# Projections dealt between the mLSTM heads, and adaLN products with the weights as stationary operand, in a hybrid decoder step

## What is computed

```
mod = silu(c) @ w_mod + b_mod            # 9 sequences, 6*1024 columns: shift, scale, gate, twice
h   = RMSNorm(x) * (1 + scale1) + shift1
z   = h @ w_in                           # conv x_c, B, C | mLSTM q, k, v, o (512 columns each) | gates i, f
y_c = B * dwconv3_causal(C * x_c)        # state: last 2 rows of C*x_c
y_m = o * mLSTM(q, k, v, i, f)           # 4 heads of 128, states C, n, m
x   = x + gate1 * ([GroupRMSNorm(y_c) | HeadRMSNorm(y_m)] @ w_out)
h   = RMSNorm(x) * (1 + scale2) + shift2
x   = x + gate2 * PEER(h)                # 8 heads, 16384 experts; then the final RMSNorm
```

## Time and profile before

| | us |
|---|---|
| median of 3 executions | 1919.88 (1917.03 to 1927.48) |
| the profiled execution | 1925.03 |
| its span in the trace | 1923.3 |
| PE busy, share of the span | 1801.0, 94% |
| DVE / ACT / POOL busy | 1368.4 / 682.4 / 1131.1 |

### The profile page before, as it was taken

The page is one execution under the profiler, slowest core; times in us unless marked ns, Lnnn a source line. Parts: engine busy times, 40 slices in busy tenths (PEclk is TensorE's granted clock), DMA queues, the critical chain, the costliest instruction groups (busy, mean ns, idle before and its releaser), DMA issues.

```text
span 1923.3 us, 27208 instructions
## 1 busy us (share of the span) xinstructions
PE 1801.0 (94%) x10594; PEld 1717.0 (89%) x10594; DVE 1368.4 (71%) x2341; ACT 682.4 (35%) x864; POOL 1131.1 (59%) x617
## 2 busy tenths in 40 slices
PE   8999985887999999999999999998999999999995
PEld 3899973576999999999999998998999999999995
DVE  2436006545789699987777877637989999999965
ACT  2453422133323333335444454433333333333331
POOL 2666622012325788865444444467878888888861
PEclk9999987978999999999999999998999999999998
DMA  8544352131204788866877787689999999999961
GB/s 315 166 147 143 131 24 98 44 105 66 89 2 130 241 275 282 277 213 209 265 241 246 239 263 246 208 315 355 391 339 369 355 362 365 353 365 355 367 208 47
DMA packets 188340, 442.74 MB, mean 230 GB/s; under 512 B 23616, under 2 KB 109632, under 8 KB 181440
## 3 DMA queue, kind: packets, MB, share of 16 engines
q1 hardware_dynamic: 79472, 252.40, 39.1%
q0 software_dynamic: 36864, 134.23, 18.8%
q10 hardware_dynamic: 71888, 54.53, 8.8%
HBM read 381.95 MB, written 59.17 MB: 229 GB/s over the span
## 4 chain that ended last, share of the span: by engine, by line
PE 83%; DVE 6%; DMA 5%; ACT 2%; ACTq 2%; issue 1%; SPq 0%; POOL 0%; DVEq 0%
PE ps L857 55%; PE ps L636 12%; PE ps L822 5%; PE ps L868 4%; ACTq L1125 2%; DMA gelu_scratch<-ga 1%; PE ps L658 1%; DMA out_conv_s<-us 1%; PE ps L685 1%; DMA tab<-in_tab 1%; ACT stage L1132 1%; PE ps L832 1%; PE ps L771 1%; DMA raw<-in_w 1%; ACT tHi L1089 1%
## 5 line engine op out<-in xcount | busy, mean ns | idle before, releaser
L592 POOL TENSOR_TENSOR tLo<-tab,tHi 128x1024 fp32r<-128x1024 f32 x256 | 637.3, 2489 | 362.8 <-ACT tHi L1089 361.3
L580 POOL TENSOR_TENSOR wLo<-raw,wHi 128x1024 fp32r<-128x1024 f32 x82 | 205.3, 2520 | 347.4 <-ACT wHi L930 347.4
L1089 ACT CAST tHi<-tab 128x1024 fp32r<-128x1024 f32 x256 | 267.9, 1047 | 390.2 <-PE ps L857 355.7
L857 PE MATMUL ps<-hHi,tLo 128*128 128x416 f32 x1024 | 368.0, 359 | 2.1 <-POOL tLo L592 1.9
L857 PE MATMUL ps<-actHi,tLo 128*128 128x416 f32 x1024 | 360.4, 352 | 9.1 <-DVE actLo L1541 9.1
L857 PE MATMUL ps<-hLo,tHi 128*128 128x416 f32 x1024 | 366.9, 358 | 0.0
L857 PE MATMUL ps<-hHi,tHi 128*128 128x416 f32 x1024 | 363.1, 355 | 0.0
L857 PE MATMUL ps<-actLo,tHi 128*128 128x416 f32 x1024 | 361.1, 353 | 0.0
L857 PE MATMUL ps<-actHi,tHi 128*128 128x416 f32 x1024 | 358.7, 350 | 0.0
L1534 DVE TENSOR_TENSOR ps<-gin,gt 128x416 f32<-128x416 f32 x128 | 199.7, 1560 | 11.3 <-DMA gt<-gate_scratch 11.3
L857 PEld LDWEIGHTS ps<-actHi,tLo 128*128 128x128 f32 x1024 | 192.8, 188 | 11.0 <-issue 7.8
(11 more groups left out here) (315 smaller groups left out, 2767.3 us busy)
## 6 DMA issues: line engine op xcount, KB each, us to landing
tab<-in_tab SPq DMA_DIRECT2D x256, 512.0 KB, 5.2
raw<-in_w SPq DMA_DIRECT2D x51, 1024.0 KB, 4.9
gelu_scratch<-ga ACTq DMA_DIRECT2D x128, 208.0 KB, 4.4
gate_scratch<-stage ACTq DMA_DIRECT2D x13, 2048.0 KB, 12.4
gt<-gate_scratch SPq DMA_DIRECT2D x32, 832.0 KB, 6.4
gin<-gelu_scratch SPq DMA_DIRECT2D x128, 208.0 KB, 4.7
xT<-in_xT SPq DMA_DIRECT2D x1, 2176.0 KB, 11.7
out_y<-yo SPq DMA_DIRECT2D x8, 272.0 KB
```

The lines of the kernel that those rows point to most:

```text
L580: pool.tensor_tensor(wLo[:, q % 2, :, half], raw[:, (NM1 + q) % RAW, :, half], wHi[:, q % 2, :, half].bitcast(F32), ALU.subtract).then_inc ...
L592: pool.tensor_tensor(tLo[:, n % SPL], tab[:, n % RAW], tHi[:, n % SPL].bitcast(F32), ALU.subtract).then_inc(s_tlo, 1)
L857: last = mm(ps[:, bank, 0:TD], w, x[:, k, 0:TD], start=first, stop=end)
L1089: nc.scalar.copy(tHi[:, n % SPL], tab[:, n % RAW]).then_inc(s_thi, 1)
```

## The change

Only the front, up to `w_out`, is reordered; every product is the same sum.

- Weights are loaded, split and freed by single units of 128 columns (512 KB), from a written-out order `STREAM`, into RAW = 5 buffers instead of four of 1 MB. `xT`, `vec` and the gate constants are loaded ahead of the first weights.
- All 48 units of `w_mod` are multiplied in plain fp32 from `raw`, with the weight tile (128x128) as stationary operand and the 9 condition columns streamed (`mod_unit`, 8 matmuls). The result is already in columns: evacuations, transposes, `c2` and the hi/lo split of 14 granules go.
- Order of PE: 16 mod units, the gate unit, then 16 times (a unit of q, k, v, o; two mod units), then the heads. The 12 conv units (x_c, C, B of tile i together) stand between the pieces of the heads, by the table `AFTER_T`, `AFTER_S`, `AFTER_D`, `AFTER_ST` (after transposes, scores, denominator, state products). They all use banks 0 and 1. The head's transposes and state products move to banks 2, 3, 4.
- The convolution of tile i is done by DVE at the end of head i (head 3: before its output is gated). The head's tiles no longer alias `hHi`, `hLo`. `mb` goes: PE broadcasts the maximum in each head and DVE reads it from PSUM. The scores now wait for `er`.
- Group sums of tile i and head i are made in head i + 1, after its scores, and PE waits for DVE to add them before the next conv unit.
- The conv states are copied to contiguous `cp`, `cs` and stored at the end; DVE no longer waits for them.

```diff
-RAW = 4
+RAW = 5
+TABS = 4
+AFTER_T, AFTER_S, AFTER_D, AFTER_ST = ([17, 21, 24, 27], [18, 22, 25, 28], [19, None, None, None], [20, 23, 26, None])
+def weight_stream():
+    order = [("mod", i) for i in range(NMA)] + [("unit", 0)]
+    for i in range(NQ):
+        order.append(("unit", 1 + i))
+        order += [("mod", NMA + 2 * i), ("mod", NMA + 2 * i + 1)]
+    return order + [("unit", n) for n in range(U_CONV, NU)]
...
+                if p >= RAW:
+                    kind, i = STREAM[p - RAW]
+                    sp.wait_ge(s_modp if kind == "mod" else s_wlo, i + 1)
                 sp.dma_start(raw[:, p % RAW], a["w"][p]).then_inc(s_raw[p % RAW], 16)
...
+            def mod_unit(i):
+                p = AT_MOD[i]
+                pe.wait_ge(s_raw[p % RAW], 16 * (p // RAW + 1))
+                bank, c = (6, NSEQ * i) if i < NMA else (7, NSEQ * (i - NMA))
+                for k in range(KT):
+                    last = mm(ps[:, bank, c:c + NSEQ], raw[:, p % RAW, k, :], cT[:, k, :], start=(k == 0), stop=(k == KT - 1))
+                last.then_inc(s_modp, 1)
+            for i in range(NMA):
+                mod_unit(i)
+                if i == NMA - 3:
+                    square_sum(0)
+            unit(0, 0, 0)
+            for n in range(1, U_CONV):
+                unit(n, max(n - 1, 0))
+                mod_unit(NMA + 2 * (n - 1))
+                mod_unit(NMA + 2 * (n - 1) + 1)
+                if n == 13:
...
             for h in range(NH):
...
+                mm(ps[:, 6, :], sel[:, h, :], row_m[:, 0:TP], start=True, stop=True)
+                mm(ps[:, 5, 320:320 + TS], sel[:, h, :], row_m[:, TP:T], start=True, stop=True).then_inc(s_bc, 1)
+                conv_unit(AFTER_T[h])
+                pe.wait_ge(s_tokc, h + 1)
+                pe.wait_ge(s_er, h + 1)
...
+                if h:
+                    pe.wait_ge(s_ev, AFTER_T[h] + 1)
+                    group_sum(h - 1)
+                    pe.wait_ge(s_gacc, h)
+                conv_unit(AFTER_S[h])
                 pe.wait_ge(s_p, h + 1)
...
+                conv_unit(AFTER_D[h])
                 pe.wait_ge(s_vw, h + 1)
+                pe.wait_ge(s_hm, h + 1)
...
+                conv_unit(AFTER_ST[h])
...
-            v.wait_ge(s_bce, NH + 1)
-            v.wait_ge(s_out, 32)
+            v.wait_ge(s_rowx, 1)
...
+                if h == NH - 1:
+                    conv(h)
+                    nc.vector.tensor_copy(cp[:], up[:, :, TP:TP + 2])
+                    nc.vector.tensor_copy(cs[:], us[:, :, :, NL:NL + 2]).then_inc(s_convout, 1)
                 v.wait_ge(s_num, h + 1)
...
+                if h < NH - 1:
+                    conv(h)
```

More of the change, by code:

```diff
@@ L72 @@
 N_GELU = NCH + 20
+AFTER_T, AFTER_S, AFTER_D, AFTER_ST = ([17, 21, 24, 27], [18, 22, 25, 28], [19, None, None, None], [20, 23, 26, None])
[5 more added lines that the diff above has]
+    return order + [("unit", n) for n in range(U_CONV, NU)]
+STREAM = weight_stream()
+AT_MOD = {i: p for p, (kind, i) in enumerate(STREAM) if kind == "mod"}
+AT_UNIT = {i: p for p, (kind, i) in enumerate(STREAM) if kind == "unit"}
 N_YT = NCH + 121
@@ L448, in load @@
                 sp.dma_start(raw[:, p % RAW], a["w"][p]).then_inc(s_raw[p % RAW], 16)
-            for p in range(NM1 + RAW + 2):
+            for p in range(AT_UNIT[1]):
                 load(p)
[L452 to L456, removed]
-            sp.dma_start(us[:, :, :, 0:2], a["sconv"]).then_inc(s_state, 16)
@@ L458, in _ @@
[L458 to L465, removed]
@@ L466, in _ @@
[L466 removed]
+            sp.dma_start(us[:, :, :, 0:2], a["sconv"]).then_inc(s_state, 16)
             sp.dma_start(n0[:], a["n0"]).then_inc(s_n0, 16)
             sp.dma_start(csb[:], a["C0"][:, 0]).then_inc(s_c0, 16)
[L469 to L473, removed]
+            p = AT_UNIT[1]
@@ L474, in _ @@
             for h in range(NH):
+                until = AT_UNIT[[26, 29, 32, 35][h]]
+                for q in range(p, until):
+                    load(q)
+                p = until
                 sp.wait_ge(s_stc, h + 1)
@@ L618, in square_sum @@
                 last.then_inc(s_nrm, 1)
[L620 to L648, removed]
+            def unit(n, free, made=None):
+                pe.wait_ge(s_wlo, n + 1)
+                if free:
+                    pe.wait_ge(s_ev, free)
+                for k in range(KT):
+                    if made is not None:
+                        pe.wait_ge(s_hlo, made + k + 1)
+                    hi, lo = wHi[:, n % 2, k, :], wLo[:, n % 2, k, :]
+                    for w, x, first, end in ((lo, hHi, k == 0, False), (hi, hHi, False, False),
+                                             (hi, hLo, False, k == KT - 1)):
+                        for h in range(2):
+                            last = mm(pair(n)[:, h], w, x[:, k, h * HF:(h + 1) * HF], start=first, stop=end)
+                last.then_inc(s_pj, 1)
@@ L742, in group_sum, with conv_unit @@
+            def conv_unit(n):
+                if n is not None:
+                    unit(n, n)
+            def group_sum(i):
+                pe.wait_ge(s_gsq, i + 1)
+                for slot, src in ((0, i), (1, CT + i)):
                     for q in range(2):
-                        last = mm(ps[0:GR, banks[q], 0:HF], fsel[:, i, :], sq[:, slot, q * HF:(q + 1) * HF],
-                                  start=(i == parts[0][0]), stop=(i == parts[-1][0]))
+                        last = mm(ps[0:GR, q, 0:HF], fsel[:, src, :], sq[:, slot, q * HF:(q + 1) * HF],
+                                  start=(slot == 0), stop=(slot == 1))
@@ L1018, in _ @@
+                    hi_part(1)
+            evacuate(0, row_li[:])
+            hi_part(2)
+            dest = (zq, zk, zv, zo)
+            for n in range(1, U_CONV):
+                kind, i = (n - 1) // 4, (n - 1) % 4
+                evacuate(n, dest[kind][:, i], ACT.Sigmoid if kind == 3 else ACT.Identity, DH ** -0.5 if kind == 1 else 1.0)
+                hi_part(n + 2)
+                if n == 4:
                     act.wait_ge(s_rowa, 1)
@@ L1301, in _, with conv, group_add @@
             tt(smp(qn[:]), smp(qwi[:]), over(n0[:], NL), ALU.mult).then_inc(s_qn, 1)
+            v.wait_ge(s_modp, NMOD)
+            mod_part(2 * KT, 6 * KT, 7)
+            link(stt(amod[:, 1], mod[:, 4 * KT:5 * KT], 1.0, over(span("g_ffn"), NSEQ), ALU.add, ALU.mult))
+            v.sem_inc(s_mods, 1)
+            def conv(i):
+                v.wait_ge(s_ev, U_CONV + 3 * (i + 1))
+                if i == 0:
+                    v.wait_ge(s_state, 16)
+                yp, ys = xc[:, i, 0:TP], xc[:, i, TP:T].rearrange("p (b l) -> p b l", l=NL)
+                tt(up[:, i, 2:2 + TP], up[:, i, 2:2 + TP], yp, ALU.mult)
+                link(tt(us[:, i, :, 2:2 + NL], us[:, i, :, 2:2 + NL], ys, ALU.mult))
+                for j in range(3):
+                    w = col("w_conv", j * CT + i)
+                    if j == 0:
+                        tsc(yp, up[:, i, j:j + TP], w, None, ALU.mult)
+                        last = tsc(ys, us[:, i, :, j:j + NL], w, None, ALU.mult)
+                    else:
+                        stt(yp, up[:, i, j:j + TP], w, yp, ALU.mult, ALU.add)
+                        last = stt(ys, us[:, i, :, j:j + NL], w, ys, ALU.mult, ALU.add)
+                    link(last)
+                tt(xc[:, i], xc[:, i], bg[:, i], ALU.mult).then_inc(s_conv, 1)
+            def group_add(i):
+                v.wait_ge(s_gst, i + 1)
+                link(tt(gv, gv, ps[0:GR, 0:2, 0:HF], ALU.add))
+                v.sem_inc(s_gacc, 1)
             for h in range(NH):
@@ L1626 @@
         "n0": i["state_mlstm_n"][0].transpose(2, 1, 0),
-        "w": np.concatenate([w_mod[:NM1], granules(gates), pairs,
-                             granules(i["w_out"][0]), granules(i["w_pq"][0])]),
+        "w": np.stack([(mods if kind == "mod" else unit)[n] for kind, n in STREAM]),
         "keys": i["sub_keys"][0].transpose(3, 1, 0, 2).reshape(P, HP, NKEY),
```

479 lines of the change are left out of this document (161 added, 318 removed).

## The result

The change makes the kernel some 2% slower: 1963.09 us (median of 4 executions, 1954.96 to 1968.55) against 1918.74 (4, 1917.03 to 1927.48); ratio 1.0198, 95% interval 1.0161 to 1.0235. The prediction was 1892 us. What came is its rival 1, which had a chance of 0.20, and its price was counted too low: 1939 us there. The profiled execution took 1960.58 us.

A forecast was written before the change was run, and what follows sets the result against it. The prediction took the part before w_out as a front of DMA and adaLN, 204 us of PE work, then a chain over PE, DVE and one DMA. Terms -5.5 - 51 + 29.5 = -27, kept -28, gave 1892 us, range 1882 to 1902.

The forecast's parts named there:

- rival 1: Clock halves under mod units: front +27 us, stretch +20, 1939 us; chance 0.20 in both places, 0.10 in front alone.
- The bound: In the stretch of units PE's work sets the time; loads keep up, the tightest with 2.3 us to spare.
- from w_out on: From w_out to the end the instructions are the same: 0 us change.
- The price of a mod unit: Each mod unit, 16 instructions with 9 streamed columns, takes 1.68 us, as L776; the other end was 3.52 from L727.
- The front: Up to the first q unit: make_h starts at 41.0 instead of 46.47 us, -5.5 us.
- The stretch: Sixteen times a unit and two mod units, plus broadcasts and transposes: 153 us against 204, -51 us.
- Heads and tail: Heads with conv units dealt between their pieces, then norms: 166 us against 136.3, +29 us.
- the group add: In heads 1 to 3 PE waits for DVE's group add: 3 us in all.
- head 3's gated output: In head 3 the convolution precedes the gated output that the state products wait for: 1.5 us of waiting.
- The 24.63 us of the store: The conv state store in the chain before the heads goes fully, contiguous copies being stored behind nothing.
- Rivals 2 and 3: DVE and POOL block each other (1903, up to 1912 us); weight stream too slow (1905 us); together chance 0.21.
- The sum: -5.5 - 51 + 29.5 = -27 us, kept as -28: 1897 from the profiled execution, 1892 against the median.

The follow-up runs named there:

- e10_before_copies: Kernel before, with only the conv states copied to contiguous buffers by DVE and stored from those: 1899.13 us, ratio 0.9851 to the kernel before.
- e8_best: Changed kernel with front mod units streamed, later ones woven into dense units, gate-row broadcasts and ones product moved: 1903.22 us, ratio 0.9894 to the kernel before.
- e11: Changed kernel, same order, all 48 mod units with conditions stationary and 128 weight columns streamed, ACT reading mod rows earlier: 1928.65 us, ratio 1.0033 to the kernel before.
- e1_woven: Changed kernel, with the 16 mod products of each pair dealt two behind each k step of the dense unit: 1929.15 us, ratio 1.0035 to the kernel before.
- e2: Changed kernel, with only the first 16 mod units in the old form, conditions stationary and weight columns streamed: 1942.86 us, ratio 1.0115 to the kernel before.
- e4_warm: Changed kernel, with 32 dense fp32 products of 288 streamed columns, results unused, added ahead of the first mod unit: 1967.97 us, one execution.
- e5_filler: Changed kernel, with a dense 288-column product, result unused, added after every second product of the first 16 mod units: 2019.19 us, one execution.

## Why the prediction was wrong

**The bound, and from w_out on: right.** PE is busy in all 190.8 us of the stretch, SP's loads keep up (one wait for `wLo`, 1.0 us, at the first unit), and from w_out on the difference is 3 us.

**The price of a mod unit: wrong, and it is the step that failed.** I took 1.68 us from L776 as nearest in shape and kept L727's 3.52 us as the other end. In the front it was 3.42. L776's 16 instructions stand alone between dense products and were over, in 1.68 us, with the clock still at 1.00; 224 in a row were not. The reading of the earlier trace rows that rival 1 made, that busy alone does not hold the clock, was the right one, and the chance of 0.20 did not do justice to it. Of the two ends, how the work stands in its surroundings should have chosen, not its shape.

**The front: 25.3 us over.** The first unit starts at 82.26 and not 56.95. Fourteen mod units took 47.93 us for 23.5 (+24.4); the ones product stands at half clock (2.01 us; 1.11 in the chain of the kernel before), and the last two mod units take 6.64 us, so the bias add comes at 67.54 instead of 41.0. Rival 1 had +27.

**The stretch: 37.8 us over, where rival 1 had 20.** The pieces of the chain, added up by kind: 32 mod units 63.6 us (1.99 each) for 53.8, so +9.8; the broadcasts and transposes 2.7 for 1.5, so +1.2; and the 16 dense units 124.6 us, 7.79 each, for 6.11: +26.8. Rival 1 charged the half clock to the mod units alone. Most of it falls on the dense unit behind them. That is the term that was missing: with it the stretch is 18 us over rival 1's 20, out of the 24 us between 1939 and 1963. Most of the rest is not the kernel's: the forecast started from a profiled execution 5.2 us over its median, and the profiled one of the change lies 2.5 us under its own.

**Heads and tail: right.** 168.0 us for 166. Part of this is luck: head 0 inherits the half clock, which the forecast did not have, and its transposes, broadcast and first unit (8.96 us for 6.20) take 4.8 us more than those of head 1. So the other terms came out 2.8 us under the forecast. PE waited for the group add 2.8 us in three heads (3 said) and 1.2 us for head 3's gated output behind the convolution (1.5 said); the rows are from the waits of PE in the kernel after:

```profile
PE ps L620 <- DVEq L1181: 2.8, 3, 0.9
PE ps L721 <- DVE zq L1219: 1.2, 1, 1.2
```

The 24.63 us of the store went. But this gain doesn't need the reordering: e10_before_copies has it with a few lines. e8_best has the copies too and is no faster, so all else in the reordering, repaired, bought nothing that these executions can tell. The 16 us expected of e10 are 20 to 28 by the medians (against the kernel before's 1918.7 and 1927.4), of which the trace shows 12.8.

**Rivals 2 and 3: hardly seen.** The masks took 0.88 us in every head. Of DVE's instructions in the chain of head 3 one was held up: the sample part of head 3's first convolution step, 2.25 us, beside its fellows of 0.17 us. Raw loads landed in 3.8 us, where 5.2 was assumed. PE was held up by POOL beside DVE in this place, 1.2 us, and at the first unit, 1.0 us (see the last section), and never by the stream.

**The sum.** 25.3 + 37.8 + 2 - 2.9 = 62 us, and the profiled execution is 63.6 us over the 1897 forecast for it; 1 us of the difference is the step from -27 to -28 in the forecast's own sum. e8_best closes the account from the other side: with the clock kept up, stretch and heads last what the forecast had, and the front is 7.8 us longer than forecast (64.78), since a mod unit costs 2.16 us there.

**What stays open.** Which property of the 9-column products lets the clock fall: their few streamed columns or their loads. e11 changes both at once. Open too is why e1_woven's mixed work regained the clock at 244 us and not before.

## What to carry to other kernels

A product with the large matrix as stationary side and a few columns streamed was cheap here only where it was short and stood among dense work. In a row it halved TensorE's clock, and in the stretch of units the dense work behind paid more (26.8 us) than the products themselves (9.8). Such products can be dealt between dense ones, as e1_woven did with two per k step, or turned round, as in e2 and e11. Before a large reordering, try alone the smallest edit that removes a wait of the chain: here contiguous copies ahead of one store gave as much as the repaired reordering.

## What the hardware showed unexpectedly

- 8 products of a 128x128 fp32 stationary tile with 9 streamed columns (16 instructions) took 1.73 us at 2.4 GHz (half of the pair's 3.47) and 3.42 us at 1.2 GHz: 0.108 and 0.214 us per instruction. L776's form with 4 columns has 1.68 and, in e10, 3.21. So 4 or 9 streamed columns make hardly a difference, which leaves the loads as what sets the price, and it doubles when the clock is halved.
- PE was busy for all of 30 us, 28 of them with such work, and stayed at half clock (e4_warm, 40 to 70 us). Mixed with dense products it was seen for long at either level: down in e5_filler until the ones product and in e1_woven for 35 us behind unit 13, up in e1_woven from 82 to 200 us.
- The clock column read 1.00 through stretches at half rate at the start of a trace: the front of the change, and e5_filler from 20 to 112 us.
- POOL's first split took 7.76 us beside DVE's fused steps of make_h, against 2.49 us on average; it ends the wait for the first unit, 1.0 us of PE's, in the change and in every repair of it.
